# First block's attention in units, with retention's projection interleaved

## The chip, the cores and the metric

One Trainium2 chip, one core. The metric is device time of one execution in microseconds, from the start of the program to its end. Engines: PE (TensorE, matmul), DVE (VectorE), ACT (ScalarE), POOL (GpSimd), SP (SyncE, issues the weight stream).

## The reference, cut to what matters

Two transformer blocks over 256 tokens of width 1024, float32. The change touches the token mixer of the first block only.

```python
h = rms_norm(x, norm_mix_pre);  proj = h @ w_in          # 256 x 2840
(rq, rk, rv, rg, nq, kcm, vcm, ksl, vsl, kwn, vwn, ng) = split(proj)
# retention, 4 heads, dk 64, dv 128 (chunks of 128 tokens, decay, group norm)
o = (rope(rq) @ rope(rk).T * decay) @ rv;   y_ret = silu(rg) * group_norm(o) * gn_w
# 8 query heads, 2 key/value groups, dk 64
kc, vc = compress(kcm), compress(vcm)                     # 15 blocks of 32 tokens, stride 16, gelu MLP
o_cmp = masked_softmax(q @ rope(kc).T) @ vc
o_slc = softmax(causal(q @ rope(ksl).T)) @ vsl            # with 4 blocks, all are selected
o_win = softmax(causal(q @ rope(kwn).T)) @ vwn            # window 512 covers all tokens
y_nsa = gate0 * o_cmp + gate1 * o_slc + gate2 * o_win     # gates = sigmoid(ng)
x = x + rms_norm(concat([y_ret, y_nsa]) @ w_out, norm_mix_post)
```

After it come a conv feed-forward, and the second block (Hyena and HGRN mixer, product-key experts).

## The kernel before

All weights come as one stream of 240 slots of 128 x 2048 floats, in two halves each (480 halves). SP loads them into a ring of six halves (lines 1137 to 1143); a half's place is loaded again when PE has counted it off in `half_multiplied`. A half is split into two fp32r parts: ACT writes the rounded part (`split`, line 1556), POOL the remainder (`rest`, line 1154), and `product` (line 1098) makes three fp32r passes of each pair of operands. Only the eight halves of the compression weights (`WHOLE`) are multiplied unsplit, as plain fp32, which shows as two records for each product. Each engine runs its own program, written out by hand; order on an engine is program order, and between engines only semaphores order. `ahead(n)` in ACT's program casts all halves up to n that aren't cast yet; `rests(a, b)` is POOL's counterpart.

PE's order in the first mixer:

1. `p1_group(0..4)` (line 1271): five groups of 512 columns of w_in: retention's queries and keys; the attention's queries; selected and window keys with the inputs of compression; retention's values; retention's gate. Each is four halves of 12 products of 512 columns, into PSUM banks 4 and 5 or 6 and 7. ACT copies the first 128 tokens to `P1`, DVE the second (`p1_copy`). The two products of the Hyena filter stand between them (`filter_product`), and their window needs two exps of 2048 elements on ACT and a product on DVE.
2. A slot of 256 columns with the selected and window values (24 products for each of 2 halves), then the products of the gates (24).
3. The rotation (rope) of 20 heads from `P1` into `R`: the first tile of tokens on POOL (lines 1188 to 1199), the second on DVE (1840 to 1845), 640 elements an operation.
4. 40 transposes, one head and one tile each, to 64 partitions (line 1330), with copies by ACT and DVE into `RT`; the duplicated inputs of compression (`DUP`, line 1338); retention's scores.
5. Compression of keys, retention's output, compression of values; the compressed branch: 16 score products of 15 columns, softmax, 16 transposes of 15 columns (line 1394), 16 products with 15 rows of values.
6. Eight attention units u (branch u // 4, tile u // 2 % 2, group u % 2): `scores` (line 1405) of four heads, `maxima` on DVE (1918), `exps` on ACT (1668), transposes (1430), copies (1682, 1948), products with the values. Scores run two units ahead. After each second unit DVE scales and adds to `mix` (1961, 1964).
7. 16 transposes of `mix` (line 1452), rounding (1569, 1770), `out_product` (line 1457) with the four slots of w_out.

Of the kernel before, what the change touches and what calls it, by code (L numbers as in the profile page):

```python
# [6 lines left out]
D = 1024  # L7
# [8 lines left out]
    0, 11, 15, 19, 52, 64, 68, 80, 84, 88, 92, 96, 100, 104, 112)  # L16
# [9 lines left out]
T_COS, T_SIN, T_DECAY, T_CAUSAL, T_KEEP, T_DROP, T_CC = 0, 64, 128, 1664, 1920, 1950, 1980  # L26
# [8 lines left out]
 out_stored half_multiplied act_step dve_step pool_step squares_summed inv_ready rstd_ready xn_ready  # L35
 xn_transposed filt_hidden filt_sine filt_window filt_product filt_ab kernel_spectrum p1_act p1_dve
 gates_product gates_ready rope_ready heads_transposed heads_act heads_dve silu_ready dup_ready dup_transposed
 blocks_ready hid_ready cmp_product vc_copied kc_ready fdecay_loaded filt_windowed filt_reduced spectrum_copied
 cmp_shifted gn_inv gn_rstd ret_normed att_rowmax ffn_tap ret_scores ret_decayed ret_out cmp_scores cmp_exp
# [13 lines left out]
def build(nc, dram):  # L53
# [8 lines left out]
    with ctx:  # L62
# [54 lines left out]
        P1 = area(4096, TOK, 2840)  # L117
        RT = area(9776, 20, SEQ)
        R = area(14896, TOK, 20, 64)
        RA, RB = area(17456, 20, 32), area(18096, 20, 32)  # L120
        RC, RD = area(18736, 20, 32), area(19376, 20, 32)
        xn = area(20016, TOK, D)
        SCR = 22064
        FH = area(SCR, TOK, 2048)
        FW = area(SCR + 4096, TOK, 2048)
        FAB = area(0, 2, TOK, D)
        DF1 = area(9776, 4, 256)
        DUP = area(SCR, TOK, 4, 2, 64)
        BLK = area(SCR + 1024, 2, 16, 30)
        HID = area(SCR + 1984, 2, 2, 30)  # L130
        HTOK = area(SCR + 8608, 2, 256)
        KCR = area(SCR + 2104, 30)
        KCT = area(SCR + 2134, 30)
        VC = area(SCR + 2164, 2, 64)
        SD = area(SCR + 2304, 4, 384)
        SM = area(SCR + 3840, 2, 4, 256)
        ET = area(SCR + 5888, 2, 1024)
        CE = area(SCR + 7936, TOK, 8, NCMP)
        CET = area(SCR + 8176, TOK * 8 * 128)
        mix = area(14896, TOK, D)  # L140
        gn = area(20016, TOK * 4, 128)
# [33 lines left out]

        def dve_copies(u):

            return 2 * (u // 4) + max(0, u % 4 - 2)


# [969 lines left out]
        def _(pool):  # L1150
# [20 lines left out]
            pool.dma_start(aux[:, 0:2040], dram["tab1"]).then_inc(S["tab_loaded"], 16)  # L1171
# [10 lines left out]
            pool.wait_ge(S["tab_loaded"], 16)  # L1182
            pool.wait_ge(S["p1_act"], 3)
            src = P1[:, 0, 0:1280].rearrange("p (h c) -> p h c", h=20)
            lo, hi = src[:, :, 0:32], src[:, :, 32:64]
            c = cosT[:, 0, :].unsqueeze(1).broadcast_to([128, 20, 32])
            s = sinT[:, 0, :].unsqueeze(1).broadcast_to([128, 20, 32])
            P.tensor_tensor(RC, lo, c, ALU.mult).then_inc(S["pool_step"], 1)  # L1188
            P.tensor_tensor(RD, hi, s, ALU.mult).then_inc(S["pool_step"], 1)
            rests(16, 18)  # L1190
            pool.wait_ge(S["pool_step"], 2)
            P.tensor_tensor(R[:, 0, :, 0:32], RC, RD, ALU.subtract).then_inc(S["pool_step"], 1)
            rests(18, 20)
            pool.wait_ge(S["pool_step"], 3)
            P.tensor_tensor(RC, lo, s, ALU.mult).then_inc(S["pool_step"], 1)
            P.tensor_tensor(RD, hi, c, ALU.mult).then_inc(S["pool_step"], 1)
            rests(20, 22)
            pool.wait_ge(S["pool_step"], 5)
            P.tensor_tensor(R[:, 0, :, 32:64], RC, RD, ALU.add).then_inc(S["rope_ready"], 1)

            pool.wait_ge(S["filt_ab"], 2)
            pool.wait_ge(S["p1_dve"], 3)
            for t in range(TOK):
                heads = P1[:, t, 1280:1536].rearrange("p (i c) -> p i c", i=4).unsqueeze(2).broadcast_to([128, 4, 2, 64])
                P.tensor_copy(DUP[:, t], heads).then_inc(S["dup_ready"], 1)
# [11 lines left out]
        def _(pe):  # L1217
# [53 lines left out]
            def p1_group(g, ready=None):  # L1271

                if g >= 2:
                    pe.wait_ge(S["p1_act"], g - 1)
                    pe.wait_ge(S["p1_dve"], g - 1)
                token_product(2 * g, 4 + 2 * (g % 2), in_parts, ready)

            p1_group(0, lambda quarter: wait_operand("norm0", 2 * quarter + 2))

            pe.wait_ge(S["filt_sine"], 1)  # L1280
            mm(ps[0:64, 0, 0:256], FT[0:64, 64:128], FHID[0:64, 0, :]).then_inc(S["filt_hidden"], 1)
            p1_group(1)
            pe.wait_ge(S["filt_sine"], 2)
            pe.wait_ge(S["w3_loaded"], 32)
# [8 lines left out]

            filter_product(0)
            p1_group(2, lambda quarter: filter_product(1) if quarter == 2 else None)
            p1_group(3)
            p1_group(4)
            pe.wait_ge(S["p1_act"], 4)
            pe.wait_ge(S["p1_dve"], 4)
            for kh in range(2):  # L1300
                w = weights(10, kh)
                for t in range(TOK):
                    for k in range(4):
                        last = product(ps[:, 6 + t, 0:256], parts(in_parts, ALL, 4 * kh + k, tile(t)),
                                       parts(w, ALL, slice(k * 256, (k + 1) * 256)), kh + k == 0, kh == 1 and k == 3)
                multiplied(last)
            pe.wait_ge(S["p1_act"], 5)
            pe.wait_ge(S["p1_dve"], 5)
            pe.wait_ge(S["gate_weights_ready"], 2)

            for k in range(KC):
                last = product(ps[0:24, 4, 0:SEQ], parts(gate_weights, ALL, k, ALL), parts(in_parts, ALL, k, ALL),
                               k == 0, k == KC - 1)
            last.then_inc(S["gates_product"], 1)


            pe.wait_ge(S["rope_ready"], 2)
            pe.wait_ge(S["filt_windowed"], 2)
            for b in range(10):
                if b >= 4:  # L1320
                    pe.wait_ge(S["heads_dve"] if b % 2 else S["heads_act"], (b - 4) // 2 + 1)
                if b == 4:

                    pe.wait_ge(S["gates_sigmoid"], 1)
                    for t in range(TOK):
                        last = nc.tensor.transpose(ps[:, 5, t * 24:(t + 1) * 24], gates_T[0:24, tile(t)], ident[0:24, 0:24])
                    last.then_inc(S["gates_transposed"], 1)
# [47 lines left out]
            for n, w2 in enumerate((w2k, w2r)):  # L1375
                for half in range(2):
                    mm(ps[0:64, 4, n * 30:n * 30 + 30], w2[:, half, :], HID[:, 0, half, :], half == 0, half == 1)
# [786 lines left out]
```

## Time and profile before

| | us |
|---|---|
| median of 3 runs | 1709.61 |
| lowest, highest | 1707.3, 1710.12 |
| profiled execution, its own time | 1711.76 |
| span of that execution's trace | 1710.0 |
| PE busy in it | 1630.0 (95%) |
| DVE, ACT, POOL busy | 1028.3, 808.8, 1208.4 |
| mean granted TensorE clock | 0.962 |

The span runs from the first to the last instruction of the trace, and the 1.8 us around it belong to the time. Busy shares are means over stages with different limits. The granted clock is a share of 2.4 GHz; 0.50 is 1.2 GHz.

### The profile page before, as it was taken

The page shows a single profiled execution, that of the slowest core. Times are in us where ns is not written, and L with a number is a line of the kernel's source. Part 1 is how long each engine was busy: PE and PEld are TensorE (multiplying, and loading weights), DVE is VectorE, ACT ScalarE, POOL GpSimd, SP SyncE. Part 2 cuts the span into 40 slices and gives each one's busy share as a digit, 9 for nine tenths or more (in the row PEclk, how much of TensorE's full clock was granted, in tenths as well). Part 3 has the DMA queues.
Part 4 walks back from the last instruction along what each step waited for, and adds up shares of the span by engine and source line. Part 5 has one row for each costly group of instructions (what it writes and reads, how often), then busy time and mean ns, then how long its engine had stood idle before and what let it go on. Part 6 is the DMA issues. An engine that isn't in the chain of part 4 may idle for free.

```text
span 1710.0 us, 31420 instructions
## 1 busy us (share of the span) xinstructions
PE 1630.0 (95%) x11688; PEld 1472.5 (86%) x11688; DVE 1028.3 (60%) x1358; ACT 808.8 (47%) x1078; POOL 1208.4 (71%) x504
## 2 busy tenths in 40 slices
PE   6888999999999999889999999999999999999997
PEld 5666779999899888888989999999999888888886
DVE  4633338666421168983415997177777999974344
ACT  5423355545655457654444444444444434444543
POOL 5830238888688595445875899877777777778995
PEclk9996599999999999988999999999999999999999
DMA  7431046555555334222654554554544455465553
GB/s 267 132 119 47 1 148 234 185 185 185 168 181 179 123 125 134 88 75 89 207 199 135 183 180 162 180 166 156 162 157 164 157 167 168 163 210 195 194 190 120
DMA packets 72629, 268.41 MB, mean 157 GB/s; under 512 B 8160, under 2 KB 8432, under 8 KB 71344
## 3 DMA queue, kind: packets, MB, share of 16 engines
q1 hardware_dynamic: 70128, 253.99, 45.2%
q0 software_dynamic: 1568, 7.66, 1.3%
q10 hardware_dynamic: 864, 5.77, 0.9%
q8 instruction: 52, 0.85, 0.2%
q14 instruction: 17, 0.14, 0.0%
HBM read 264.24 MB, written 3.15 MB: 156 GB/s over the span
## 4 chain that ended last, share of the span: by engine, by line
PE 38%; issue 25%; POOL 25%; DVE 5%; ACT 4%; DMA 2%; POOLq 0%; SPq 0%; DVEq 0%; ACTq 0%
PE ps L1095 38%; POOL ring_lo L1154 24%; DMA ring<-in_stream 2%; DVE big L859 1%; ACT ring_hi L1556 1%; DVE big L858 1%; DVE big L884 1%; ACT big L600 0%; ACT big L605 0%; DVE big L857 0%; ACT big L630 0%; DVE big L868 0%; DVE big L860 0%; ACT h_hi L1569 0%; POOL big L1188 0%
## 5 line engine op out<-in xcount | busy, mean ns | idle before, releaser
L1154 POOL TENSOR_TENSOR ring_lo<-ring,ring_hi 128x1024 fp32r<-128x1024 f32 x472 | 1183.7, 2523 | 479.8 <-ACT ring_hi L1556 478.7
L1556 ACT CAST ring_hi<-ring 128x1024 fp32r<-128x1024 f32 x472 | 489.7, 1050 | 479.2 <-DMA ring<-in_stream 476.9
L1095 PE MATMUL ps<-h_hi,ring_hi 128*128 128x256 f32 x2144 | 616.5, 288 | 8.3 <-POOL ring_lo L1154 5.0
L1095 PE MATMUL ps<-h_lo,ring_hi 128*128 128x256 f32 x2144 | 610.3, 285 | 0.0
L1095 PE MATMUL ps<-h_hi,ring_lo 128*128 128x256 f32 x2144 | 610.1, 285 | 0.0
L1095 PEld LDWEIGHTS ps<-h_hi,ring_hi 128*128 128x128 f32 x2144 | 414.7, 193 | 12.8 <-issue 9.2
L1095 PEld LDWEIGHTS ps<-h_lo,ring_hi 128*128 128x128 f32 x2144 | 414.7, 193 | 0.8 <-issue 0.5
L1095 PEld LDWEIGHTS ps<-h_hi,ring_lo 128*128 128x128 f32 x2144 | 414.5, 193 | 0.0
L1095 PE MATMUL ps<-ring_hi,h_hi 128*128 128x512 f32 (+1 forms) x672 | 266.6, 397 | 14.8 <-POOL ring_lo L1154 8.9
L1095 PE MATMUL ps<-ring_hi,h_lo 128*128 128x512 f32 (+1 forms) x672 | 262.1, 390 | 0.0
L1095 PE MATMUL ps<-ring_lo,h_hi 128*128 128x512 f32 (+1 forms) x672 | 261.8, 390 | 0.0
L1095 PE MATMUL ps<-big 128*128 128x128 f32 (+10 forms) x780 | 169.2, 383 | 33.5 <-DVE big L868 8.2
L1095 PEld LDWEIGHTS ps<-big 128*128 128x128 f32 (+4 forms) x780 | 132.6, 234 | 66.0 <-issue 39.0
L1770 DVE TENSOR_TENSOR h_lo<-big,h_hi 128x512 fp32r<-128x512 f32 (+1 forms) x65 | 123.7, 1905 | 102.0 <-ACT h_hi L1569 102.0
L1095 PEld LDWEIGHTS ps<-ring_hi,h_hi 128*128 128x128 f32 x672 | 127.8, 190 | 44.5 <-issue 19.9
L1095 PEld LDWEIGHTS ps<-ring_hi,h_lo 128*128 128x128 f32 x672 | 127.6, 190 | 26.4
L1095 PEld LDWEIGHTS ps<-ring_lo,h_hi 128*128 128x128 f32 x672 | 127.9, 190 | 24.8
L1048 DVE TENSOR_TENSOR big<-ps,big 128x512 f32 (+1 forms) x64 | 86.6, 1353 | 88.3 <-PE ps L1095 49.8
L1029 DVE TENSOR_TENSOR onehots_i<-routes,ps 128x1024 bf16<-128x1024 f32 (+1 forms) x64 | 77.5, 1211 | 0.0
L715 ACT ACTIVATE big<-ps 128x512 f32 (+1 forms) x64 | 38.3, 598 | 82.8 <-PE ps L1095 82.6
L2000 DVE SCALAR_TENSOR_TENSOR big<-ps,vecs,big 128x255 f32<-128x255 f32 (+1 forms) x88 | 36.4, 473 | 51.0 <-ACT big L1723 51.0
L1037 DVE TENSOR_TENSOR onehots_j_even<-onehot_j,ps 128x1536 bf16<-128x1536 bf16 x32 | 56.1, 1754 | 4.4
(313 smaller groups left out, 1552.6 us busy)
## 6 DMA issues: line engine op xcount, KB each, us to landing
ring<-in_stream SPq DMA_DIRECT2D x480, 512.0 KB, 3.6
residual<-big ACTq DMA_DIRECT2D x2, 1024.0 KB, 4.0
big<-residual ACTq DMA_DIRECT2D x2, 1024.0 KB, 7.9
x<-in_x SPq DMA_DIRECT2D x1, 1024.0 KB, 5.6
big<-in_fdecay POOLq DMA_DIRECT2D x1, 1024.0 KB, 9.4
wrow<-in_post POOLq DMA_DIRECT2D x2, 512.0 KB, 6.5
big<-in_x ACTq DMA_DIRECT2D x1, 1024.0 KB, 5.0
big<-in_dft POOLq DMA_DIRECT2D x1, 1024.0 KB, 10.1
```

The source lines that it names most:

```text
L715: A.activation(H[:, bass.ds(j, 2), :].rearrange("p a b -> p (a b)"), ps[:, (52 + s) % 3, :], ACT.Gelu_apprx_tanh).then_inc(S["h_ready"], 1)
L858: V.tensor_tensor(keys[:, :, 1, :], kb[:, :, 1, :], d_first, ALU.subtract).then_inc(S["level_shifted"], 1)
L859: V.tensor_tensor(queries[:, :, 0, :], d_first, d[:, :, 0, :], ALU.subtract).then_inc(S["level_shifted"], 1)
L884: last = V.copy_predicated(AT[hg][:, :, st, st * 128:(st + 1) * 128], mask, ps[:, 4 + 2 * (n % 2) + st, :].rearrange("p (h c) -> p h c", h=4))
L1029: V.tensor_tensor(OA[:, q % 2], first.unsqueeze(2).broadcast_to([128, 8, 128]), IOTA.unsqueeze(1).broadcast_to([128, 8, 128]), ALU.is_equal)
L1037: V.tensor_tensor(OB[q % 2][:, :, :, :], ONEHOT_J[:, :, :].unsqueeze(1).broadcast_to([128, 3, 8, 64]), GATE_PARTS[:, :, bass.ds(tok, 8)].u ...
L1048: V.tensor_tensor(h, ps[:, bank, :].rearrange("p (t j) -> p t j", t=8), h, ALU.mult).then_inc(S["gated"], 1)
L1095: return nc.tensor.matmul(out, lhsT, rhs, start=start, stop=stop, skip_group_check=True)
L1154: P.tensor_tensor(ring_lo[:, h % RING, :], ring[:, h % RING, :], ring_hi[:, h % RING, :].bitcast(fp32), ALU.subtract).then_inc(S["split_lo ...
L1556: A.copy(ring_hi[:, h % RING, :], ring[:, h % RING, :]).then_inc(S["split_hi"], 1)
L1770: V.tensor_tensor(lo, src, hi.bitcast(fp32), ALU.subtract).then_inc(S["operand_lo"], 1)
L2000: V.scalar_tensor_tensor(y, ps[:, i % 4, j * 256:j * 256 + 256 - s], vecs[:, bass.ds(col, 1)], y, ALU.mult, ALU.add).then_inc(S["ffn_tap"] ...
```

## The change

The w_in columns are ordered anew: compression inputs with selected and window keys, then the queries, then retention's queries and keys. Retention's values and gate (1024 columns) are cut into four slots of 256 columns and moved behind the compression weights in the stream. PE multiplies them in eight pieces (one tile of tokens each), between the parts of the attention units. Units are now numbered tile first (tile u // 4, branch u // 2 % 2, group u % 2). Query heads are stored in pairs (one of each group), so one transpose of 128 columns turns two heads, and the two groups lie on partitions 0 to 63 and 64 to 127 of `RT`; w_out's rows and the gates' columns follow. DVE rotates both tiles straight from PSUM, in place; the inputs of compression are copied from PSUM by ACT. Compressed keys are laid out block-diagonally over the two groups (`KCT`), the compressed values over eight heads (`VC`, 120 rows), so that a tile needs four score products, one transpose and one product of 512 columns. The filter's bias and its two additions go from DVE to POOL. Group norm works in PSUM, its squares on ACT.

```diff
-    0, 11, 15, 19, 52, ...
+    0, 7, 15, 19, 52, ...                    # W_IN, W_CMP, W_OUT, ...
+A_KV, A_QUERIES, A_RET, A_VALUES, A_RV = 0, 2, 4, 6, 11
@@ pool
-            rests(8, 16)
...
-            P.tensor_tensor(RC, lo, c, ALU.mult).then_inc(S["pool_step"], 1)
...
+            rests(8, WHOLE[0])
+            pool.wait_ge(S["filt_windowed"], 2)
+            P.memset(FH[0:1, 0, D:2 * D], 0.0).then_inc(S["filt_edge"], 1)
+            P.tensor_tensor(FH[0:1, 0, 0:D], FH[0:1, 0, 0:D], wrow[0:1, :], ALU.add).then_inc(S["filt_edge"], 1)
+            pool.wait_ge(S["filt_edge"], 2)
+            P.tensor_tensor(FAB[:, 0], FH[:, :, 0:D], FH[:, :, D:2 * D], ALU.add).then_inc(S["filt_ab"], 1)
+            P.tensor_tensor(FAB[:, 1], FH[:, :, D:2 * D], FH[:, :, 0:D], ALU.subtract).then_inc(S["filt_ab"], 1)
+            rests(WHOLE[1], 2 * W_OUT)
@@ tensor
+            def narrow_product(n, bank, t):
+                w = [weights(n, half) for half in range(2)]
+                for half in range(2):
+                    for k in range(4):
+                        last = product(ps[:, bank, t * 256:(t + 1) * 256], parts(in_parts, ALL, 4 * half + k, tile(t)), ...)
+                    if t:
+                        multiplied(last)
+            token_product(A_KV, 4, in_parts, ...)
+            token_product(A_QUERIES, 6, in_parts)
+            filter_product(0)
+            pe.wait_ge(S["dup_ready"], 2)
+            pe.wait_ge(S["rope_ready"], 1)
+            token_product(A_RET, 4, in_parts, lambda quarter: filter_product(1) if quarter == 3 else None)
...             # 8 DUP transposes, narrow_product(A_VALUES, 0, t), gates, compress(0, 0..3)
+            for j in range(5):
+                for p in (2 * j, 2 * j + 1):
+                    for t in range(TOK):
+                        last = nc.tensor.transpose(ps[:, (4 + j) % 8, ...],
+                                                   R[:, t, 2 * p:2 * p + 2, :].rearrange("p h c -> p (h c)"), ident[:, :])
...             # compress(1, 0..1), retention scores, compress(1, 2..3)
+            scores(0)
+            hidden_transposed(0)
+            hidden_transposed(1)
+            for u in range(8):
+                if u < 7:
+                    scores(u + 1)
+                if u == 0:
+                    retention_part(0, 0)
+                probabilities(u)
+                if u == 0:
...                 # compressed keys and values
+                    retention_part(0, 1)
+                if u == 1:
...                 # compressed scores
+                    retention_part(1, 0)
+                if u == 2:
+                    retention_part(1, 1)
...                 # transposes of the compressed probabilities
+                if u == 3:
+                    retention_part(2, 0)
+                    pe.wait_ge(S["cmp_pcopied"], 1)
+                    for t in range(TOK):
+                        last = mm(ps[:, 6 + t, :], CET[0:120, tile(t)], VC[0:120].rearrange("p h c -> p (h c)"))
+                if u == 4:
+                    retention_part(2, 1)
+                if u == 5:
...                 # retention's output
+                    retention_part(3, 0)
+                if u == 6:
+                    retention_part(3, 1)
+                attended(u)
@@ scalar
-            A.activation(P1[:, :, 2048:2560], P1[:, :, 2048:2560], ACT.Silu).then_inc(S["silu_ready"], 1)
+            for u in range(8):
+                if u < 7:
+                    exps(u + 1)
+                act.wait_ge(S["att_transposed"], u + 1)
+                A.copy(ET[:, u % 2, 0:512], ps[:, 0 if u >= 4 else u % 2, :]).then_inc(S["att_copied_act"], 1)
...                 # part_copied(i) and ahead(two more halves) at u = 0, 2, 4, 6
+                if u == 5:
+                    A.activation(gn2, ps[:, 6:8, :]..., ACT.Square).then_inc(S["ret_squared"], 1)
+                if u == 6:
...                 # Sqrt of group norm, then Silu of the gate
@@ vector
+            def rotary(bank, first, count, col):
+                V.tensor_tensor(ra, lo, c, ALU.mult)
+                step(V.tensor_tensor(rb, lo, s, ALU.mult))
+                step(V.tensor_tensor(lo, hi, s, ALU.mult))
+                V.tensor_tensor(R[:, :, first:first + count, 0:32], ra, lo, ALU.subtract)
+                step(V.tensor_tensor(hi, hi, c, ALU.mult))
+                V.tensor_tensor(R[:, :, first:first + count, 32:64], rb, hi, ALU.add).then_inc(S["rope_ready"], 1)
+            rotary(4, 0, 4, 256)      # before reduce_angle(.., 1)
+            rotary(6, 4, 8, 0)        # before the filter's window products
+            rotary(4, 12, 8, 0)       # after the blocks of compression
+            maxima(4)                 # order on DVE, second half of the units:
+            branch(1)
+            copied(4)
+            maxima(5)
...             # two additions of the compressed branch into mix
+            copied(5)
+            maxima(6)
+            branch(2)
...             # group norm: sums, means, centring
+            copied(6)
+            maxima(7)
...             # group norm: variance, weight
+            copied(7)
...             # group norm: scaling, product with the gate
+            branch(3)
```

## Rows read from the trace of the kernel before

**Rows 1.** The page: granted clock in 40 slices of 42.75 us, tenths.

```profile
PEclk9996599999999999988999999999999999999999
```

**Rows 2.** Stages, all engines: start:end, length, busy of each, clock, DMA, GB/s.

```profile
103.00:132.00 29.00, 25.88 (x158) 17.43 (x155) 15.01 (x20) 7.42 (x12) 0.00 (x0) 1.00 0.38 128
132.00:157.00 25.00, 19.07 (x114) 17.12 (x114) 9.33 (x28) 7.17 (x16) 0.00 (x0) 0.67 0.11 40
157.00:213.00 56.00, 51.50 (x193) 43.32 (x194) 20.94 (x81) 23.22 (x72) 14.09 (x6) 0.50 0.00 0
...
219.30:240.00 20.70, 20.70 (x92) 16.98 (x91) 1.37 (x3) 6.86 (x9) 11.93 (x5) 1.00 0.65 216
682.00:688.00 6.00, 4.99 (x43) 4.83 (x42) 6.00 (x10) 4.46 (x5) 1.33 (x1) 1.00 0.49 175
...
216.30:1710.00 1493.70, 1449.13 (x10864) 1329.59 (x10862) 931.48 (x1180) 726.59 (x926) 1119.00 (x454) 0.98 0.50 164
```

**Rows 3.** PE timeline to 125 us: start, length, instruction, idle before.

```profile
41.04 3.70 PE L1095 MATMUL ps<-big 64*128 64x512 f32 x8
48.38 0.77 PE L1095 MATMUL ps<-ring_hi,h_hi 128*128 128x512 f32 x1 [3.64 <-POOL ring_lo L1154]
...
84.11 0.47 PE L1095 MATMUL ps<-ring_hi,h_hi 128*128 128x512 f32 x1 [2.01 <-POOL ring_lo L1154]
...
93.01 0.55 PE L1095 MATMUL ps<-ring_hi,h_hi 128*128 128x256 f32 x1 [2.96 <-POOL ring_lo L1154]
...
96.12 0.28 PE L1095 MATMUL ps<-ring_hi,h_lo 128*128 128x256 f32 x1
96.24 0.28 PE L1095 MATMUL ps<-ring_hi,h_hi 128*128 128x256 f32 x1
...
106.69 2.81 PE L1330 MATMUL ps<-identity,big 128*64 128x128 f32 x24
...
110.36 2.85 PE L1095 MATMUL ps<-big 64*128 64x256 f32 x16
114.76 7.09 PE L1095 MATMUL ps<-ring,big 128*30 128x256 f32 x32 [1.54 <-DVE big L1862]
121.78 2.95 PE L1095 MATMUL ps<-big 128*128 128x128 f32 x24
```

**Rows 4.** PE timeline from 133 us: compressed branch, units, output transposes.

```profile
134.23 4.46 PE L1095 MATMUL ps<-big 64*128 64x15 f32 x32 [0.58 <-DVE big L1887]
140.95 3.34 PE L1394 MATMUL ps<-identity,big 128*15 128x128 f32 x16 [2.26 <-DVE big L1898]
146.23 9.84 PE L1095 MATMUL ps<-big 15*128 15x64 f32 x48 [1.94 <-ACT big L1666]
...
158.38 5.68 PE L1095 MATMUL ps<-big 64*128 64x256 f32 x16
...
212.94 3.67 PE L1452 MATMUL ps<-identity,big 128*128 128x128 f32 x16 [1.58 <-DVE big L1964]
```

**Rows 5.** Weight loads on PE in the attention.

```profile
162.09 1.78 PEld L1095 LDWEIGHTS ps<-big 128*128 128x128 f32 x8 [0.65 <-issue]
```

**Rows 6.** DVE timeline.

```profile
59.34 2.29 DVE L1823 TENSOR_TENSOR big<-ps,big 128x2048 f32<-128x2048 f32 x1 [12.15 <-PE ps L1095]
...
73.69 3.01 DVE L1841 TENSOR_TENSOR big<-big,aux 128x640 f32<-128x640 f32 x1
...
189.84 0.42 DVE L1928 CUSTOM_DVE_ANT_0 big<-ps,aux 128x256 f32<-128x256 f32 x1 [1.54 <-PE ps L1095]
...
206.88 0.69 DVE L1948 COPY big<-ps 128x512 f32<-128x512 f32 x1 [6.31 <-PE ps L1430]
```

**Rows 7.** ACT timeline.

```profile
133.96 1.28 ACT L1662 ACT_TABLE_LOAD   x1
...
164.41 0.49 ACT L1675 ACTIVATE big<-big,stat 128x256 f32<-128x256 f32 x1
```

**Rows 8.** POOL timeline.

```profile
28.28 7.14 POOL L1154 TENSOR_TENSOR ring_lo<-ring,ring_hi 128x1024 fp32r<-128x1024 f32 x3
```

More of the change, by code:

```diff
@@ L1269, in _ @@
             norm_transposes(0)
[L1271 to L1284, printed above, removed]
+            def narrow_product(n, bank, t):
+                w = [weights(n, half) for half in range(2)]
+                for half in range(2):
+                    for k in range(4):
+                        last = product(ps[:, bank, t * 256:(t + 1) * 256], parts(in_parts, ALL, 4 * half + k, tile(t)),
+                                       parts(w[half], ALL, slice(k * 256, (k + 1) * 256)), half + k == 0, half == 1 and k == 3)
+                    if t:
+                        multiplied(last)
             def filter_product(pt):
@@ new lines, in _ @@
+            pe.wait_ge(S["gates_sigmoid"], 1)
+            for t in range(TOK):
+                last = nc.tensor.transpose(ps[:, 1, t * 24:(t + 1) * 24], gates_T[0:24, tile(t)], ident[0:24, 0:24])
+            last.then_inc(S["gates_transposed"], 1)
+            compress(1, 0)
+            compress(1, 1)
+            pe.wait_ge(S["heads_act"], 3)
+            pe.wait_ge(S["heads_dve"], 2)
+            for h in range(4):
+                rows = slice(h % 2 * 64, h % 2 * 64 + 64)
+                queries, keys = RT[rows, 6 + h // 2, :], RT[rows, 8 + h // 2, :]
+                mm(ps[:, 4 + h, 0:256], keys[:, 0:128], queries)
+                mm(ps[:, 4 + h, 256:384], keys[:, 128:256], queries[:, 128:256]).then_inc(S["ret_scores"], 1)
@@ new lines, in _, with scores @@
+            compress(1, 2)
+            compress(1, 3)
+            def scores(u):
+                qt, br, g = u // 4, u // 2 % 2, u % 2
+                nk = 128 * (qt + 1)
+                if u >= 2:
+                    pe.wait_ge(S["att_rowmax"], 4 * (u if qt else u - 1))
+                rows = slice(g * 64, g * 64 + 64)
+                for r in range(4):
+                    col = r * nk
+                    last = mm(ps[:, 4 + (col // 512 if qt else u % 2), col % 512:col % 512 + nk],
+                              RT[rows, 2 + r, qt * 128:(qt + 1) * 128], RT[rows, br, 0:nk])
+                last.then_inc(S["att_scores"], 1)
@@ L1935, in maxima, with into_mix @@
                                 ALU.mult).then_inc(S["att_max"], 1)
-            maxima(0)
+            def into_mix(t, source, rec, first):
+                out = mix[:, t, 512:1024].rearrange("p (h c) -> p h c", h=8)
+                heads = source.rearrange("p (h c) -> p h c", h=8)
+                if first:
+                    return V.tensor_tensor(out, heads, over(rec, 8, 64), ALU.mult)
+                step(V.tensor_tensor(heads, heads, over(rec, 8, 64), ALU.mult))
+                return V.tensor_tensor(out, out, heads, ALU.add)
```

588 lines of the change are left out of this document (268 added, 320 removed).

## The prediction

> **What bounds the kernel now.** I read the page's slices first: PE is busy nearly everywhere, and the granted clock is full in nearly every slice, but not in the stretch of the first block's attention: there it falls to 6, 5 and 5 tenths [rows 1]. So the question is not the busy share but the level of the clock and what PE does at it. The table by stage gives that [rows 2]: from 157 to 213 us PE is busy 51.5 of 56 us at 0.50, which is the 1.2 GHz level; no DMA runs, ACT is busy 23 us and DVE 21. In the two stages before (103 to 132, 132 to 157) 9 of 54 us are idle. From 216.3 us on the out projection and everything behind it run at 0.98 (1449 of 1494 us busy); the diff touches nothing there but the order of columns in the weights. Hence everything is decided by when the out projection starts, 216.3 us today. I take the last 1493.7 us as unchanged; the ring holds its six halves at that point today and would again.
>
> The PE timeline then says what moves the clock [rows 3, 4]. After an idle gap of 3.64 us (to 48.38) the first record lasts 0.77 us, where it is 0.47 at 84.11, and those behind it 0.63 for 0.39 until 51.5; the same after 2.96 us (93.01 to 95.9), while a gap of 2.01 us leaves it alone. Each time some 3 us of dense fp32r products bring it back, at 216.26 too. In the compressed branch 32 tiny products start at full clock and the transposes behind them run at half. The attention between, 56 us nearly without idle, never brings it back: plain fp32 products and transposes alone do not lift it here, though fp32 products hold it where it is up (110 to 132, window at 1.00).
>
> **The change, part by part.** I walk PE's new order from 29.4 us, the end of the first projection group, which is unchanged. Lengths are start to start: a dense product of 512 columns takes 0.225 us (92 in 20.7) [rows 2], so the 12 of a weight half 2.73 with the handover; one of 256 columns 0.12, so 24 take 2.88 [rows 3].
>
> *Lead, to the end of the third group.* Group 2 runs to 41.6 as now (11 us), the first filter product to 45.3 (3.7). The rotation of the first four heads (six DVE operations of 256 elements at 0.42, from the 0.69 for 512 [rows 6], 2.5 us) comes ahead of the sine reduction, which takes 7.1 us now, so the second sine ends at 40.3 instead of 37.7, still before PE wants it. In return ACT casts halves 8 and 9 before the table load and the two 2 us exps: POOL has half 8 at 45.8 and not 48.25, so the 3.64 us gap shrinks to 0.5. Halves 10 and 11 are cast behind the exps (49.6), PE waits 1.8 for half 10; with 4 x 2.73 and the second filter product, 3.7, the group ends at 62.2. Today 65.0: 2.8 us gained. If the reduction is slower by 2 us, so is all behind it.
>
> *To the first attention unit.* Duplicate transposes 0.95; the value projection 5.76 (48 x 0.12); gates 2.8; compression twice 7.09; 20 head transposes instead of 40, at 0.12 (2.4 instead of 4.8); gate transposes 0.3; retention scores 2.85 [rows 3]. Sum 29.2, so 91.4 us. Hidden beside it: the rotation of 8 heads, six operations of 0.72 over two tiles (4.3 us), twice, done 16 and 7 us before PE needs it; it replaces the 640-element operations, 2.2 to 3.0 us on DVE [rows 6] and up to 3.7 on POOL, which end at 87.6 and 96.7 now and are late for nothing either, except that POOL's last two halves wait behind them. POOL gets the filter's two 2048-element additions: by its 2.38 us for 1024 [rows 8] 4.7 each, 12.5 us with the small ones, from 62 to 75 us; DVE asks for them at 92 and POOL's next half is cast at 83. Cover 17 and 8 us, so nothing.
>
> *The attention.* Work on PE at full clock: scores of a unit are 8 records. At half clock they last 3.7 us at 256 columns (158.38 to the first weight load of the values, 162.09), so 1.75 (an estimate: half, less the handover), and 0.95 at 128; transposes 0.12 each, 4 or 8; attended values 1.78 for 8 records at half clock, so 1.0 for 8 and 1.84 for 16 [rows 3 to 5]. Four units of each kind: 10.8 + 6.0 + 11.4 = 28.2 us. The retention values and gates, 21.8 us in two groups now, become eight pieces of 2.88 = 23.0 (1.2 more, since each stationary load serves 256 columns). Retention output 2.95. The compressed branch: transposes of 15 columns, 16 now in 3.34, become 2 (0.3); its values, 48 records in 9.84 us at half clock, become two fp32 products of 512 columns, four records at the filter product's 0.46 (8 in 3.70), 1.8; its scores 16 records instead of 32, 1.3; with the small ones 5.5 in all where 24 us pass now (131.7 to 156.1) [rows 3, 4]. Sum 59.6.
>
> *Waits left.* Per unit the chain is scores, four row maxima (0.21 or 0.35 each, then 0.25), four exps (0.39 or 0.49), copy 0.57 [rows 6, 7]: 4.2 us for a one-tile unit. PE has 0.95 + 2.88 + 0.53 = 4.4 beside it: covered. For a two-tile unit it is 1.75 + 1.65 + 2.0 + 0.6 = 6.0 against 5.6. And DVE and ACT have more queued: two results of the compressed branch put behind maxima of unit 5 (unit 4 waits 2.3); branch 2 and the centring of retention (1.42 + 2.68) ahead of the copy and the maxima of unit 7 (unit 6 waits 3.7); cast of two halves, two table loads of 1.28 [rows 7] and silu ahead of ACT's copy for unit 7 (waits 4.1). Together 10.1. So the last attended product ends at 91.4 + 59.6 + 10.1 = 161.1. Then branch 3 (1.7, as now), transposes 1.9 at full clock (3.67 now [rows 4]), rounding 1.9: the out projection would start at 166.6, at full clock throughout.
>
> The weights of the eight pieces: halves 22 and 23 are split by 88; each later pair needs two casts (2.0) and two remainders (4.8) [rows 7, 8] and lies ready 3 to 30 us before its piece. POOL and DMA idle there now, so nothing.
>
> *The clock.* The 3.7 and 4.1 us waits are as long as the ones that dropped it. So unit 6's values, unit 7 and the output transposes (6.5 us at full) take nearly twice as long: +6.3. Unit 4's wait of 2.3 lies between the 2.01 that did nothing and the 2.96 that did: half of a 3 us loss, +1.5. Start 174.4, that is 41.9 before today's. Bounds: 0 extra (166.6), or half clock for all work after 91.5 us, eight pieces included: 59.6 x 0.9 = 54 more, less the 8 us of waits that this fills, about 212. I take the near end because pieces of 2.88 us stand between all units, because a later stretch of mixed work holds 1.00 with 1 us of 6 idle (682 us) [rows 2], and because each dense run in the rows lifted it.
>
> Two rules of the Trainium skill bear on this. DVE operations that read two SBUF tensors wait here while POOL works: 640 elements take 3.01 us where 2048 from PSUM take 2.29 with POOL busy [rows 6]. The page SBUF — State Buffer, section on the two sides and the shared pair of ports, says that the loser of the pair fully blocks. It speaks against the additions moved to POOL, but between 62 and 75 us DVE has only operations fed from PSUM; the sum stays. The page TensorE: Matmul & The Clock Gate, Part 3, says that weight loads overlap with running products when row groups differ; two heads per transpose puts retention's heads on alternate halves of the array, and by it the 2.85 us could be nearer 1.5. No row shows it.
>
> **Sum.** The profiled execution has a span of 1710.0 and took 1711.8. 1711.8 - 41.9 = 1669.9; it stands 2.2 above the median, so against medians 1709.6 - 41.9 = 1668 us.
>
> **Rivals.**
> *Half clock holds in the attention.* For: attention has been at 1.2 GHz for 56 us with PE busy; pieces are short, and plain fp32 work outweighs them (28 + 8 against 23 us). Against: each dense run of [rows 3] lifted it. At half clock for all of it the start is 212, time 1705; for half of the work 190, time 1683.
> *Slower: the clock is lost earlier and the pieces pay for it.* Compression, transposes and retention scores hold 1.00 now behind the dense gates product. If PE falls to 1.2 GHz at 71.7 us, waiting for the blocks of tokens, and never recovers, 19.7 us of work ahead of the units doubles, and with 212 behind it the start is 231 and the time 1724. It decides once over 4.3 us are lost ahead of the units in the half-clock case (216.3 less 212). Against: the blocks are ready at 67.5, four before need.
> *ACT becomes the bound.* In the units ACT does exps 14, copies 4.6 + 3.0, casts 14, three small ones: 40 of 70 us, all in order. If each copy is 1 us later than reckoned, 8 us: 1676, a variant inside the forecast.
> *The change doesn't do what it says*: the projection ends up beside nothing and only the smaller branch saves. Compressed branch 17 us less, transposes 2.4: about 1690.
>
> **How the numbers follow.** Forecast with its variants, ACT's included: 0.72, between 1656 (no drop, a chain a few us shorter) and 1680. Partly at half clock: 0.10, about 1683. Only small savings: 0.06, 1690. All at half clock: 0.07, 1705, of which 0.02 comes out as no change. Slower: 0.05. Range 1656 to 1692, which leaves out 0.12 above and about 0.05 below. A difference of 0.2% (3.4 us) is what can be told from none: faster 0.93, same 0.02, slower 0.05.
>
> **What would show it.** In the profile after: the granted clock of 91 to 150 us near 1.00 with short dips; out projection's first product near 174 us; the third group's end near 62; first unit's scores near 91; waits of 2 to 4 us ahead of the attended products of units 4, 6 and 7 by ACT's copy; two 512-column products at about 0.46 a record where 48 stood; POOL's additions of 2048 elements at 4.7. Wrong: a clock of 0.50 across the units, a wait for ring_lo before a piece, DVE waiting for POOL's additions, or a time behind the out projection's start that isn't 1493.7 within 3 us.

## The result and the profile after

The changed kernel takes 1662.18 us (median of 4 runs, 1658.17 to 1663.66) against 1709.86 us for the kernel before (4 runs, 1707.3 to 1711.65) beside it: a ratio of 0.972, 95% interval 0.9699 to 0.9741. It is faster by 2.8%, some 48 us. The forecast was 1668 us. The profiled execution took 1663.66 us, its span is 1661.8 us; before it was 1711.76 and 1710.0.

The page's granted clock in 40 slices of 41.5 us, to be read against [rows 1]: the slices at 6 and 5 tenths (the fourth and fifth) are gone, and a single 8 is left where they were.

```profile
PEclk9998999999999999999999999999999999999999
```

The stages, in the columns of [rows 2]. The first five lines cut the span at the first attention unit, at the edges of the two dips of the clock, and at the out projection. The last four are stretches of 4 us inside these dips.

```profile
91.00:132.00 41.00, 38.05 (x299) 34.54 (x298) 23.52 (x78) 23.07 (x69) 14.19 (x6) 1.00 0.28 94
132.00:140.00 8.00, 8.00 (x35) 6.73 (x35) 0.94 (x2) 1.73 (x2) 4.66 (x2) 0.58 0.06 25
140.00:157.00 17.00, 13.89 (x111) 13.12 (x110) 10.27 (x30) 7.34 (x21) 0.00 (x0) 0.99 0.20 63
157.00:171.00 14.00, 9.81 (x48) 9.23 (x48) 5.95 (x9) 8.87 (x12) 9.33 (x4) 0.51 0.01 1
171.00:1662.00 1491.00, 1446.22 (x10865) 1327.65 (x10863) 926.67 (x1181) 727.45 (x926) 1118.23 (x454) 0.99 0.49 164
...
136.00:140.00 4.00, 4.00 (x17) 3.29 (x16) 0.94 (x2) 0.00 (x0) 1.52 (x1) 0.50 0.00 0
140.00:144.00 4.00, 4.00 (x36) 4.00 (x36) 1.60 (x11) 2.54 (x9) 0.00 (x0) 0.98 0.02 4
...
160.00:164.00 4.00, 1.43 (x7) 1.43 (x7) 3.33 (x5) 3.99 (x5) 2.40 (x2) 0.50 0.02 4
164.00:168.00 4.00, 2.43 (x12) 2.24 (x12) 1.39 (x2) 0.40 (x1) 4.00 (x2) 0.50 0.00 0
```

The attention stage of before had 0.50 for 56 us [rows 2]; now 58 of the 80 us between 91 and 171 stand at full clock, and 22 in the two dips (0.58 and 0.51).

PE's timeline after, in the order of the prediction's walk (start, length, instruction, idle before and what ended it), to be read against [rows 3, 4]:

```profile
53.35 0.47 PE L1089 MATMUL ps<-ring_hi,h_hi 128*128 128x512 f32 x1 [1.39 <-POOL ring_lo L1148]
...
62.81 1.04 PE L1279 MATMUL ps<-identity,big 128*128 128x128 f32 x8
72.32 7.09 PE L1089 MATMUL ps<-ring,big 128*30 128x256 f32 x32
79.34 2.40 PE L1310 MATMUL ps<-identity,big 128*128 128x128 f32 x20
...
85.48 1.68 PE L1089 MATMUL ps<-big 64*128 64x256 f32 x16
...
90.66 1.16 PE L1089 MATMUL ps<-big 64*128 64x128 f32 x8
...
119.67 1.88 PE L1089 MATMUL ps<-big 120*128 120x512 f32 x4
122.43 3.03 PE L1089 MATMUL ps<-big 128*128 128x64 f32 x16 [0.87 <-ACT big L1686]
...
131.41 5.71 PE L1089 MATMUL ps<-big 128*128 128x64 f32 x24 [2.08 <-ACT big L1686]
137.05 1.97 PE L1354 MATMUL ps<-identity,big 128*128 128x128 f32 x8
138.81 3.50 PE L1089 MATMUL ps<-big 128*128 128x128 f32 x24
...
155.83 2.41 PE L1089 MATMUL ps<-big 128*128 128x64 f32 x16 [3.11 <-ACT big L1686]
...
162.57 3.68 PE L1089 MATMUL ps<-big 128*128 128x64 f32 x16 [2.62 <-ACT big L1686]
...
167.81 3.45 PE L1450 MATMUL ps<-identity,big 128*128 128x128 f32 x16 [1.57 <-DVE big L1918]
...
171.02 0.48 PE L1089 MATMUL ps<-ring_hi,h_hi 128*128 128x512 f32 x1
```

The first unit's scores stand at 90.66 (before at about 152), the four copies that PE waits for stand at units 3, 4, 6 and 7, and the out projection begins at 171.02 instead of 216.26: 45.2 us of the span's 48.2 are won by then.

### The profile page after: what moved, and what is told of

The parts are those of the page before. It is cut to its first block, busy times and chain, and to the rows that moved or that the text cites. A ratio compares the mean times of both kernels' runs of the same rounds, so it can differ in the third digit from the quotient of the medians.

```text
span 1661.8 us, 31456 instructions
## 1 busy us (share of the span) xinstructions
PE 1593.0 (96%) x11710; PEld 1445.9 (87%) x11710; DVE 1014.3 (61%) x1359; ACT 807.6 (49%) x1077; POOL 1202.4 (72%) x500
## 4 chain that ended last, share of the span: by engine, by line
PE 83%; DVE 6%; ACT 5%; issue 3%; DMA 2%; POOL 2%; SPq 0%; DVEq 0%; POOLq 0%; ACTq 0%
PE ps L1089 82%; POOL ring_lo L1148 2%; DMA ring<-in_stream 1%; DVE big L853 1%; ACT ring_hi L1554 1%; DVE big L852 1%; DVE big L878 1%; ACT big L624 0%; DMA vecs<-in_vecs 0%; DVE big L851 0%; DVE big L854 0%; ACT big L1673 0%; DVE big L862 0%; ACT h_hi L1567 0%; PE ps L1216 0%
## 5 line engine op out<-in xcount | busy, mean ns | idle before, releaser
L1089 PE MATMUL ps<-ring_hi,h_hi 128*128 128x512 f32 (+1 forms) x704 | 271.3, 385 | 5.5 <-DVE h_lo L1795 1.7
L1089 PE MATMUL ps<-ring_hi,h_lo 128*128 128x512 f32 (+1 forms) x704 | 266.6, 379 | 0.0
L1089 PE MATMUL ps<-ring_lo,h_hi 128*128 128x512 f32 (+1 forms) x704 | 266.2, 378 | 0.0
L1089 PE MATMUL ps<-big 128*128 128x128 f32 (+9 forms) x740 | 144.8, 356 | 36.3 <-ACT big L1686 8.7
L1089 PEld LDWEIGHTS ps<-big 128*128 128x128 f32 (+3 forms) x740 | 110.6, 208 | 64.1 <-issue 34.4
L1089 PEld LDWEIGHTS ps<-ring_hi,h_hi 128*128 128x128 f32 x704 | 133.0, 189 | 32.3 <-issue 7.3
L1089 PEld LDWEIGHTS ps<-ring_hi,h_lo 128*128 128x128 f32 x704 | 132.9, 189 | 25.3
L1089 PEld LDWEIGHTS ps<-ring_lo,h_hi 128*128 128x128 f32 x704 | 133.2, 189 | 23.6
L1031 DVE TENSOR_TENSOR onehots_j_odd<-onehot_j,ps 128x1536 bf16<-128x1536 bf16 x32 | 56.1, 1754 | 4.4
```

The costliest lines, as they stand in the source:

```text
L1031: V.tensor_tensor(OB[q % 2][:, :, :, :], ONEHOT_J[:, :, :].unsqueeze(1).broadcast_to([128, 3, 8, 64]), GATE_PARTS[:, :, bass.ds(tok, 8)].u ...
L1089: return nc.tensor.matmul(out, lhsT, rhs, start=start, stop=stop, skip_group_check=True)
```

## The experiments

My theory: TensorE's clock decides the attention, and the pieces of retention's projection between the units hold it up and fill PE's waits; the smaller compressed branch gives the rest. First rival: the smaller branch alone gives it. Second rival: waits alone give it, and the level of the clock costs little.

**1. The pieces ahead of the units.** All else of the change stays; the eight pieces run in one block before the first unit, in two banks in turn, and ACT's copies of them go there too.

```diff
+            for i in range(4):
+                for t in range(TOK):
+                    retention_part(i, t)
             for u in range(8):
...
-                if u == 0:
-                    retention_part(0, 0)
...
```

> The changed kernel, with the eight pieces of retention's projection all ahead of the attention units (banks 3 and 2 in turn) instead of between them; same work. Theory (the pieces between the units keep the granted clock up): the clock falls to 0.50 in the units, their 37 us of PE work take some 70, the out projection starts near 194 us and the time is 1682 to 1690. Rival (the clock does not hang on the pieces; a unit's own work keeps it, and the pieces are only cover): clock near 1.00, 24 us of pieces and then units bound by the chain of maxima, exps and copies, start at 174 to 178, time 1665 to 1669.

Measured: 1690.4 us (4 runs, 1686.82 to 1690.72), ratio to before 0.9871, 0.9837 to 0.9905. Stages and waits of PE in this kernel (waits: total us, times, longest), and its first out projection product:

```profile
90.00:122.00 32.00, 27.80 (x236) 26.70 (x235) 2.80 (x22) 12.38 (x25) 14.14 (x6) 1.00 0.47 152
122.00:201.00 79.00, 61.44 (x256) 51.90 (x257) 33.26 (x98) 31.38 (x81) 13.97 (x6) 0.61 0.03 7
```

```profile
PE ps L1089 <- ACT big L1683: 15.6, 6, 6.0
PE ps L1089 <- POOL ring_lo L1148: 4.0, 2, 3.3
PE ps L1444 <- DVE big L1908: 1.6, 1, 1.6
PE ps L1422 <- DVE big L1952: 0.5, 1, 0.5
```

```profile
198.48 0.78 PE L1089 MATMUL ps<-ring_hi,h_hi 128*128 128x512 f32 x1
```

By the two out projection starts, the change without its interleaving wins 216.3 - 198.5 = 17.8 us, and the interleaving 198.5 - 171.0 = 27.5 us. Of these I can split the second: the same products run from the first scores to the out projection in 108.7 us here (89.80 to 198.48) and 80.4 us in the changed kernel; waits are 21.7 us here, 8.7 + 1.6 = 10.3 there. So 11.4 us are waits: 6.9 more for ACT's copies, 4.0 in which the pieces wait for their own weights when they come in one block, and 0.5 for DVE. The other 17 us are the level of the clock, 0.73 over these 108.7 us against 0.87 over 91 to 171 in the changed kernel. Two things were not as I expected. The out projection starts at 198.5 and not near 194. And the clock did not stay at half in the units: it came back twice without any dense product near, from 150.0 to 156.8 and from 170.4 to 180.6 us.

The prediction's rival that only the smaller branch saves said 1690 for a kernel without the overlap, and that is what this one takes. The agreement is partly luck: the rival's 17 us for the branch held 3.8 us that are not the branch's (shown further down), and it had no term for the shorter lead. That the smaller branch gives most of the 17.8 us is argued from lengths; no run changes it alone.

**2. The kernel before, with dense products added and nothing else.** They multiply the operands of the first projection (the expectations call them filter operands), 256 columns each, into a free bank, and nobody reads the results: 48 once (the diff), or in every unit 24, or 12.

```diff
+            def dense(count):
+                for k in range(count):
+                    mm(ps[:, 4, 0:256], h_hi[:, k % KC, 0:128], h_hi[:, (k + 1) % KC, :])
...
+                if u == 0:
+                    dense(48)
+                pe.wait_ge(S["att_exp"], 4 * u + 4)
```

> The kernel before, with one run of 48 dense fp32r products of 256 columns (into bank 4, overwritten) ahead of the first unit's transposes; 5.8 us at full clock. Theory: the run lifts the clock, and the units' plain fp32 work lets it fall again within a unit or two; time 1709 to 1716, clock near 0.55 from 165 to 213 us. Rival (what fp32 work finds, it keeps): the clock stays at 1.00 after the run, the units take about 30 us instead of 56, time 1685 to 1692.

> The kernel before, with a run of 24 dense fp32r products of 256 columns ahead of the transposes of each of the eight units: 23 us of added work at full clock, 46 at half. Theory: the clock is at 1.00 over nearly all of the units, and PE's 51.5 us become 26 + 23; time 1700 to 1712, so 23 us of added work cost nothing. Rival (short runs do not lift it among fp32 work): 0.50 throughout, time 1745 to 1755.

> The kernel before, with 12 dense bf16-rate products of 256 columns (filter operands, results never used) in each of the eight attention units, after the unit's compressed scores and ahead of its wait for the exponentials; the run with 24 a unit took 3.11 us a unit and was no longer than the kernel before, with the clock up in 157-213. Theory (the attention of the kernel before is long because the clock stands at half): half the dense work, 8 x 1.5 = 12 us less than the run with 24, still keeps the clock near 1.00 in 157-213, so the time is 1709.9 - 12 = about 1698 (1694 to 1702), faster than before by 8 to 12 us. Rival (12 a unit are too few to hold it): the clock is at 0.50 for most of 157-213 and the added work is paid at half clock, 1712 to 1735. Second rival (the clock is not what makes the attention long, the 24 products were hidden in waits): no change against the run with 24, 1708 to 1712.

Measured: once 1714.92 us, ratio 1.002 (1.0001 to 1.0039); 24 a unit 1709.92 us, ratio 0.9998 (0.9976 to 1.0019); 12 a unit 1702.61 us, ratio 0.9959 (0.994 to 0.9977). The stage 157 to 213 us with 24 a unit, and then with 12, each to be read against the third line of [rows 2]:

```profile
157.00:213.00 56.00, 53.51 (x388) 49.55 (x387) 20.18 (x92) 25.00 (x78) 14.13 (x6) 0.94 0.00 1
```

```profile
157.00:213.00 56.00, 48.65 (x313) 43.74 (x314) 25.37 (x89) 27.72 (x82) 14.13 (x6) 0.89 0.02 5
```

The clock goes from 0.50 to 0.94 and 0.89, and the kernel with 12 is 7 us *shorter* than the one without them (its out projection starts at 211.03, not 216.26), although it has 96 products more. With 24 a unit, 23 us of work for nothing cost nothing that the ratio shows (0.9998); in the profiled execution the out projection starts at 218.56, 2.3 us later than before. One run of 48 lifts the clock at 167.9 us, the attention loses it at 178.1 again, and the kernel is longer by 0.2%, with an interval that begins at 1.0001. That settles the second rival's question: the level of the clock is worth about 20 us here. The 23 us of added work came in for 2.3 us at the most, and PE idles 2.5 us in these 56 now and 4.5 before, so only 2 of them lie in waits. And in this kernel one run is not enough; it has to be renewed between the units. My number for 12 was 8 to 12 us; it is 7 with an interval of 4 to 10, since the clock still fell twice (0.89, where I had reckoned with 1.00).

**3. Two small parts undone.** The compressed values in 16 products of 64 columns instead of two of 512, and the retention heads in an order in which neighbours lie in the same half of the array's rows.

```diff
-            for h in range(4):
+            for h in (0, 2, 1, 3):
...
-                        last = mm(ps[:, 6 + t, :], CET[0:120, tile(t)], VC[0:120].rearrange("p h c -> p (h c)"))
+                        for h in range(8):
+                            last = mm(ps[:, 6 + t, h * 64:(h + 1) * 64], CET[0:120, tile(t)], VC[0:120, h, :])
```

> The changed kernel with two parts undone: the compressed values in 16 products of 64 columns (still 120 rows) instead of 2 of 512, and retention's scores in the order of heads 0, 2, 1, 3, so that neighbours sit on the same half of the array. If a product's price is its weight load and count, 32 records at 0.12 last 3.9 us instead of 1.88; and if the 1.6 us of retention's scores come from heads on alternate halves, two of the three changes of half go and they last 2.5 to 2.9 us. Time +1 to +3.5 us. Rival: both are what they are by columns, and nothing moves.

Measured: 1660.92 us (4 runs), ratio 0.9708, 0.9672 to 0.9745, no different from the change; I had expected 1 to 3.5 us more. Its two groups on PE (the second holds, behind 32 records of the values, 8 of unit 3's attended values and 8 of unit 5's scores):

```profile
85.06 2.33 PE L1089 MATMUL ps<-big 64*128 64x256 f32 x16
...
119.91 6.50 PE L1089 MATMUL ps<-big 120*128 120x64 f32 x48
```

The scores take 2.33 instead of 1.68 us, so alternation between the halves is what makes them short; the values take about 3.5 instead of 1.88 (the attended values behind them start at 123.43). Of these 2.3 us, 0.9 are gone at once, because unit 3 waited 0.87 us for ACT's copy and now does not. The out projection begins at 171.78, that is 86.7 us after retention's scores for 85.5 in the changed kernel, so some 1.2 us are still there at that point. Whether they reach the end can't be told: the intervals of the two ratios are wider than that.

**4. The two dips of the clock, and the order on ACT and DVE.** First, dense products in the waits: 12 before the attended values of units 4 and 6, 16 before unit 7's, 12 before the last transposes:

```diff
+                if u in (4, 6):
+                    pe.wait_ge(S["att_done"], u // 2)
+                    dense(2, 12)
+                if u == 7:
+                    pe.wait_ge(S["p1_act"], 5)
+                    dense(3, 16)
...
+            dense(3, 12)
```

Second, ACT and DVE do unit 6's and 7's weights ahead of retention's group norm (on ACT the Square now stands behind the copy of unit 6, Sqrt and Silu and the cast of two weight halves behind that of unit 7; on DVE the centring and the last gate product move back likewise). Third, both.

```diff
-                if u == 5:
-                    act.wait_ge(S["ret_centred"], 1)
-                    A.activation(gn2, ps[:, 6:8, :].rearrange("p a (h c) -> p (a h) c", h=4), ACT.Square).then_inc(S["ret_squared"], 1)
...
+                    act.wait_ge(S["ret_centred"], 1)
+                    A.activation(gn2, ps[:, 6:8, :].rearrange("p a (h c) -> p (a h) c", h=4), ACT.Square).then_inc(S["ret_squared"], 1)
```

> The changed kernel, with dense products (filter operands, 256 columns, results never used) where TensorE waits before the attended values of units 4 and 6 (12 each), of unit 7 (16) and before the transposes of the mixed values (12). Theory (the two stretches at half clock, 133.3 to 140.1 and 157.2 to 170.6 us, cost time): the clock holds 1.00 in both, the out projection begins 3 to 7 us earlier, total 1655 to 1659 against some 1661. Rival (the stretches at half clock hold mostly waits for the copies and VectorE's chain, which full clock doesn't shorten, and the added products push behind the waits): no change to 2 us longer, 1660 to 1664.

> The changed kernel with another order on two engines: ScalarE copies the weights of units 6 and 7 before the square and the square root and Silu of the retention group norm, and VectorE centres and scales the retention output after the copies of unit 6 and the maxima of unit 7, and does the last branch sum before the last gate product. Theory (the waits before the attended values of units 6 and 7, 3.11 and 2.62 us, come from the retention chain that stands ahead of the copies on these two engines): the two waits fall together by 3 us or more, the out projection begins near 167 instead of 171, total 1656 to 1658. Rival (the retention chain must be done before the mixed transposes either way, so that what is taken from the waits of the units comes back in front of the transposes): 1660 to 1662, with a longer idle before the transposes than 1.57 us.

> The changed kernel with the dense products and the other order at once. Theory (both cost time, and independently in part): 1653 to 1657. Rival (what sets the end of this stage is the chain of VectorE and ScalarE alone): no shorter than the run with the other order alone.

Measured: dense products 1657.53 us, ratio 0.9691 (0.9665 to 0.9717); order 1659.63 us, 0.9708 (0.9686 to 0.9731); both 1657.46 us, 0.9688 (0.9662 to 0.9715). These differences are near what can be told, so the changed kernel and the one with dense products ran once more side by side, 5 rounds each.

> The changed kernel itself, unaltered, beside the next one on the same chip and against the same runs of the kernel before. Every theory: 1658 to 1664, the ratio 0.970 to 0.974 as before.

> The kernel with the dense products in the waits once more, the same code. Theory (it is 5.9 us earlier at the out projection and 4 to 6 us shorter in all): 1654 to 1658, ratio lower than that of the changed kernel by 0.002 to 0.004. Rival (its 4.6 us in the medians were scatter between calls): the two ratios are within 0.001 of each other.

Measured: changed kernel 1661.98 us, ratio 0.9722 (0.9703 to 0.974); with dense products 1655.16 us, ratio 0.9686 (0.9665 to 0.9707). Both times the dense products give a ratio lower by 0.003 to 0.004, that is 5 to 6 us. In their profile (the second execution) the same stages as above read:

```profile
132.00:140.00 8.00, 8.00 (x64) 7.43 (x62) 2.54 (x12) 3.04 (x8) 4.66 (x2) 1.00 0.11 42
140.00:157.00 17.00, 15.33 (x112) 14.55 (x111) 8.73 (x20) 9.27 (x21) 2.82 (x2) 0.92 0.21 63
157.00:171.00 14.00, 13.37 (x86) 11.74 (x85) 7.14 (x11) 7.84 (x11) 6.59 (x3) 0.98 0.35 126
```

```profile
129.35 1.60 PE L1089 MATMUL ps<-h_hi 128*128 128x256 f32 x12
131.59 3.92 PE L1089 MATMUL ps<-big 128*128 128x64 f32 x24 [0.64 <-ACT big L1699]
...
163.03 1.97 PE L1463 MATMUL ps<-identity,big 128*128 128x128 f32 x16
165.20 0.47 PE L1089 MATMUL ps<-ring_hi,h_hi 128*128 128x512 f32 x1 [0.19 <-POOL ring_lo L1148]
```

The dip at 132 to 140 is gone, the one from 157 on is a short one at 154 to 157.5, and the out projection starts at 165.20 in this execution and 165.16 in the first. The changed kernel's started at 171.02 and, run again, at 168.58: its dips don't lie at the same place in each execution (the second time 124.9 to 128.3 and 152.1 to 169.2 us). So 52 products whose results nobody uses win 3.4 to 5.9 us net, and the dips cost at least that. This is the fastest version, with or without the other order.

The order alone shifts a wait. In that kernel units 6 and 7 wait 2.14 and 1.54 us instead of 3.11 and 2.62, and then:

```profile
165.50 3.68 PE L1450 MATMUL ps<-identity,big 128*128 128x128 f32 x16 [2.70 <-DVE big L1998]
```

The transposes wait 2.70 instead of 1.57 us for the retention gate, now last on DVE; half of the 2 us gained is given back, and the start at 168.83 is within the changed kernel's own two (168.58, 171.02). With dense products it adds nothing (start 165.79). I had expected 3 us or more from the two waits; the rival has it.

## Why the prediction came out as it did

The sum was 41.9 us won before the out projection and nothing behind it. Measured are 45.2 and 2.9 us. Two readings of before's rows were off without any effect on the sum: [rows 1] have a 6 and one 5, not two; and the first filter product starts at 41.04 [rows 3], not 41.6, but what PE waited for behind it was POOL. Step by step:

- **Lead.** Forecast: third group done at 62.2, POOL waits of 0.5 (half 8) and 1.8 (half 10). Measured: duplicates from 62.81, no wait for half 8, 1.4 us for half 10. The execution itself began 1.4 us later (first norm transposes 11.75, before 10.32), and its first ten dense products lasted 0.63 us each where before's lasted 0.39; so the step is 0.8 us better than forecast.
- **To the first unit.** Forecast 29.2 us, measured 90.66 - 62.81 = 27.9. Compression 7.09 and head transposes 2.40 stand as reckoned; the retention scores are the difference, 1.6 us start to start for 2.85. They were mis-sized in the sum. The prediction had the reason beside it, as a rule of the Trainium skill (TensorE: Matmul & The Clock Gate, Part 3): weight loads overlap with running products when the row groups differ. Its own estimate from that was "nearer 1.5"; the trace agrees (1.68), and experiment 3 shows the cause, with 2.33 when neighbours share a half. POOL's two additions took 4.63 and 4.57 us for my 4.7, and PE waited for nothing from 60 to 122 us.
- **The attention.** Forecast from first scores to last attended product: 59.6 work, 10.1 waits, 1.5 + 4.4 for the clock (6.3 less the 1.9 of the last transposes), 75.6 us. Measured 166.24 - 90.66 = 75.6 us. The waits are where they were forecast but for a small one more: unit 4 2.08 (forecast 2.3), unit 6 3.11 (3.7), unit 7 2.62 (4.1), unit 3 0.87 (0), 8.7 in all. Work I take from the kernel with dense products: 161.27 - 90.83 = 70.4, less 3.5 waits and 5.8 of those products, is 61.1 with a short dip in it. So the clock cost the changed kernel some 75.6 - 8.7 - 61.1 = 5.8 us. That the totals agree to 0.1 us is luck: the work was 1.5 us more than forecast and the waits 1.4 us less. The compressed values took 1.88 us for 1.8. On the side of before I misread a row: the 48 records of [rows 4] at 146.23 are not all compressed values. Grouped by line and shape (busy us, mean ns), the last third are the scores of the first two units:

```profile
L1095 PE MATMUL ps<-big 15*128 15x64 f32 x32 | 6.1, 376 | 1.9 <-ACT big L1666 1.9
L1095 PE MATMUL ps<-big 64*128 64x128 f32 x16 | 3.8, 428 | 0.0
```

So "24 us pass now" for the compressed branch held 3.8 us of attention. The forecast's sum, which adds up the new order, has no term from it; the rival of 1690 had one.
- **Behind the last attended product.** Forecast 1.7 + 3.8 (transposes at half clock) + 1.9 (rounding) = 7.4, measured 171.02 - 166.24 = 4.8: 1.57 and 3.2 us, and the rounding is hidden. This step failed in its size: at half clock the rounding of one part runs beside the transposes of the next, as [rows 4] had it already (transposes from 212.94, out projection at 216.26, nothing between). I had added a term that only full clock shows: there the transposes take 1.97 us and PE waits 0.85 for h_lo in the kernel with both edits.
- **Behind the out projection's start.** Forecast 1493.7, unchanged; measured 1490.8. Of these 1.3 us lie ahead of the second norm's transposes (246.28 before, 199.76 now, 46.5 us earlier): the out projection starts at full clock, a product of 0.48 instead of 0.78 us, which the forecast counted neither way. (In the second profiled execution of the changed kernel it starts at half clock, 0.78 us, so this part comes and goes.) The other 1.6 us I don't explain; profiles of kernels alike behind this point have 1485.0 to 1491.6 us there.

The sum of the slips is 3.4 before the out projection and 2.9 behind, 6.3 us, and the forecast for the profiled execution, 1669.9, was 6.2 above its 1663.66. The mechanism held, and the rivals fell: no stage is at 0.50 but the dips, nothing between the first group and the units lost the clock in the profiled execution, ACT is in four waits and not in eight.

One reading was wrong all the same. "Plain fp32 products and transposes alone do not lift it here" was read from 56 us of one stage. In the changed kernel PE does only attended values, scores, transposes and retention's output (138.81) from 131.41 to 142.06, and the clock is back at 140.2, ahead of the next piece; it rises at 170.9 too, within the last transposes. In experiment 1 it came back twice among such work, and even in the kernel before it stood at full from 143.9 to 147.3, in the compressed branch. What experiment 2 supports is less: the mix of before's attention did not bring the clock back in 56 us, and dense products among it do. The Trainium skill (TensorE: Matmul & The Clock Gate, Part 1) has the clock follow how busy PE has been; the trace does not bear that out as it stands, with PE busy 51.5 of 56 us at 0.50 [rows 2]. I can't say from these runs what the right rule is.

The forecast of where the clock falls rested on the length of PE's gaps (2.01 us did nothing, 2.96 us did). The long waits do stand before the second dip, but a long gap is not needed: in the second profiled execution of the changed kernel the clock fell at 124.9 us with no gap over 0.87 us since the first scores, and in the kernel before it fell at 137.1 us, with no gap over 0.58 us in the 22 us ahead of it. So the place of the dips was forecast with some luck, and only their cost is confirmed.

## What to carry to other kernels

Read the granted clock by stage before the busy share: a stage of small fp32 products can be busy and at half clock, and then independent dense products put between its parts are nearly free, or less than free. Test it first with products that nobody reads; if the kernel gets no longer (here 23 us of them cost nothing in the whole time, and 12 a unit won 7 us), it pays to bring real work there, which gave 27 us. A short part saved in front of a wait for another engine is saved only beyond that wait (0.9 of 2.3 us went into it here): look at what the next instruction waits for.

## What the runs showed of the hardware beyond that

Small DVE operations stood still until an operation of POOL was done. DVE and POOL of the changed kernel (start, length, instruction):

```profile
44.07 1.95 DVE L1853 CAST gate_weights_hi<-big 128x192 fp32r<-128x192 f32 x1 [3.77 <-DMA big<-in_gnw]
...
98.99 2.32 DVE L1947 TENSOR_TENSOR big<-big 64x15 f32<-64x15 f32 x1
...
118.00 1.79 DVE L1908 TENSOR_SCALAR stat<-stat 128x4 f32<-128x4 f32 x1
```

```profile
43.57 4.71 POOL L1148 TENSOR_TENSOR ring_lo<-ring,ring_hi 128x1024 fp32r<-128x1024 f32 x2 [3.48 <-ACT ring_hi L1554]
...
96.55 4.74 POOL L1148 TENSOR_TENSOR ring_lo<-ring,ring_hi 128x1024 fp32r<-128x1024 f32 x2 [6.73 <-ACT ring_hi L1554]
...
117.37 2.39 POOL L1148 TENSOR_TENSOR ring_lo<-ring,ring_hi 128x1024 fp32r<-128x1024 f32 x1
```

64x15 elements end at 101.31 and POOL's pair at 101.29; 128x4 elements end at 119.79 and POOL's operation at 119.76 (it takes 0.17 us at 110.94, when POOL rests). The gate weights' cast took 0.25 us before, with POOL idle. The Trainium skill (SBUF — State Buffer, section on the two sides and the shared pair of ports) says that the loser waits for the whole instruction; the trace agrees, also for operations with one small source. The prediction weighed it for the additions only; the lead and the compressed branch lost up to 2.3 us on DVE at each such place. At one of them PE paid. The operation at 118.00 is the last step of unit 4's maxima, and ACT waits for it before its four exps and the copy that unit 3's attended values need:

```profile
119.83 0.51 ACT L1673 ACTIVATE big<-big,stat 128x256 f32<-128x256 f32 x1 [3.65 <-DVE stat L1908]
...
121.81 0.56 ACT L1686 COPY big<-ps 128x512 f32<-128x512 f32 x1
```

PE goes on at 122.43, after the 0.87 us for which the forecast had nothing. With 0.17 us for that operation the copy would be done some 1.6 us earlier, before PE is free at 121.55 (an estimate; no run tests it). At the other places PE did not wait; that cover was there by luck and not by my sum.
